# Splitting product 5 of a fast matrix product once more in the eight convolution groups

## The chip, the cores and the metric

The kernel runs on one core of a Trainium2 chip. The metric is the device time of one execution in microseconds. A profile of one execution gives the start and length of each instruction on each engine: PE (TensorE, the matmuls), DVE (VectorE), ACT (ScalarE), POOL (GpSimd) and SP (SyncE, which issues most of the DMAs). DMAs that add into their destination are issued by POOL.

## The reference, cut to what matters

```python
h = rmsnorm(x, norm_g)                       # x: 1024 tokens x 1024
proj = h @ w_in                              # 1024 x 12288
b_a, c_a, x_a, z_a, q, k, v, z_b, g_a, g_b = split(proj)
u = conv3(c_a * x_a) + conv_b                # causal, depthwise, three taps
y_a = (b_a * u * silu(z_a)) @ w_a_out
y_b = retention(q, k, v, z_b) @ w_b_out
out = rmsnorm(x + (sigmoid(g_a) * y_a + sigmoid(g_b) * y_b) @ w_o, final_g)
```

All in float32. The change concerns `h @ w_in` for the channels of the convolution branch.

## The kernel before, in words

**The product.** Each float32 operand is held as two parts, a high one rounded to the matmul's format and a low one, what is left. A product is three matmuls: high by high, high by low, low by high. `h @ w_in` is made in 2 value groups and then 20 channel groups `g` of 512 channels each: two gate groups (0, 1), eight conv groups (`CONVS`, 2 to 9), eight turn groups (`QZS`, 10 to 17: queries, keys and their gates) and two gate groups (18, 19). A channel group multiplies by a scheme with seven products of half-size matrices in place of eight (Winograd's form of Strassen's), in the order `ORDER = (1, 6, 2, 5, 7, 3, 4)`. The sums of x that it needs are made once and kept in `hc`, high and low; the sums of the weights are made for each group. A full product is 24 matmuls of 512 columns (`unit`). Products 4 (in groups 1 to 18) and 3 (in conv groups, `THIRDS`) are themselves made by the same scheme with seven quarter products: 42 matmuls of 256 columns, as `first_half` (three quarter products, 18 matmuls) and `second_half` (four, 24 matmuls). Below, 3a and 3b are the halves of product 3, 4a and 4b those of product 4. In a conv group PE does 1, 6, 2, 5, 7, 3a, 4a, 4b, 3b.

**The parts of x for a halved product.** `second_part` gives the four sums T1, T2, T3, T4. For product 4 three of them lie in `hx`, for product 3 in `third_parts`; T3 takes the place of a quarter in `hc`, and the quarter is brought back from HBM when the halved groups are over.

**Weights.** The four blocks of a group's weights (512 KB each) come into five buffers `work`, with the roles a to e of `ROLES`. SyncE loads a, b, c and d. POOL makes S1 = b + d in e (L934), S2 = a + S1 in a (L944), and S3 and S4 by adding DMAs from HBM (L939, L950). In a halved product `second_sums` makes four quarter sums in place on POOL: L957, L958, L960, L962. Each unit of work, a product or a half, has one of three `slots`: ACT copies the weights into it as the high part (`high(u)`, L1146), DVE subtracts for the low part (`low(u)`, L1678 or, without a sign change, L1681; called the split of the unit below), and PE waits for it (`w_ready`). `high(u)` waits until PE is through with unit u - 3. A first half has 768 columns of weights, all else 1024.

**Sums of the products.** Product 1 is copied out of PSUM by ACT; DVE subtracts each of 6, 5, 7, 3 and 4 (`add`, L1828 and L1830). Of a halved product DVE first does `second_first` (L1836, 256 columns, after the first half), then the three steps of `second_rest` (L1849: 768, 512 and 512 columns), then `add`. PE needs a product's bank back two products later: 3 waits for the sum of 5, 7 for the reader of 2.

**A conv group's tail.** When group g - 1 was a conv group, the work of its channels runs beside group g. ACT makes sigmoids and `first_tap`; POOL multiplies three gates (`conv_gate`: L980, L976, L983); DVE does `conv_product` for both halves (L1901, L1904), two `conv_tap` (L1909) and `conv_y` (L1916). DVE's `conv_early` (L1894, the gate product) multiplies a half of product 2 with its sigmoid straight out of PSUM, and PE's product 7 waits for it. ACT's copies out of product 2 wait for `conv_y` of the group before.

**The order** is written out by hand: each engine has a loop over the units u, and places each step by group and by place p of the unit in its group. Each engine works strictly in its own order. DVE in a conv group behind a conv group, before: at the start split 6, rest of 3, its `add`, L1901, split 2, L1904; then split 5; after product 6 `add`, taps, y, split 7; after 2 split 3a and the gate product; after 5 `add` and split 4a; after 7 `add` and split 4b; after 3a and 4a their `second_first`, split 3b and split 1 of the next group; after 4b its rest and `add`.

## Time and the profile before

| | us |
|---|---|
| median of 3 runs | 1365.0 (1364.61 to 1365.46) |
| the profiled execution | 1365.87 |
| its span, first to last instruction | 1364.1 |
| PE busy | 1351.8 |
| DVE, ACT, POOL busy | 1060.0, 608.3, 413.7 |

The granted TensorE clock is full nearly throughout (mean 0.998). Matmuls are pipelined, so the length shown for one (0.39 us for 512 columns) is more than the distance to the next (0.227 us). Conv groups lie between 238 and 536 us of the span.

### The profile page before, as it was taken

What the parts mean: (1) busy time and instruction counts of PE and PEld (TensorE: products, weight loads), DVE (VectorE), ACT (ScalarE), POOL (GpSimd) and SP (SyncE); (2) the same over time, 40 slices, a digit from 0 to 9 for tenths busy, and PEclk for the clock granted to TensorE, in tenths of its full rate; (3) what the DMA queues carried; (4) which work ended last, traced back from release to release, by engine and by line L of the source; (5) the groups of instructions that cost most, each with busy time, mean ns of one, the idle gap of its engine ahead of it and who ended that gap; (6) DMA issues with size and microseconds to landing.
All of it is one profiled execution on the core that took longest, in us unless ns stands there. A gap on an engine that the chain in (4) does not pass through costs nothing.

```text
span 1364.1 us, 17294 instructions
## 1 busy us (share of the span) xinstructions
PE 1351.8 (99%) x6642; PEld 1142.7 (84%) x6642; DVE 1060.0 (78%) x1097; ACT 608.3 (45%) x821; POOL 413.7 (30%) x381
## 2 busy tenths in 40 slices
PE   9999999999999999999999999999999999999997
PEld 7788888888888888888888888888888888888886
DVE  6898465677878777678888778748776998788887
ACT  6843233433333333333333433438778433433445
POOL 0100112344444554444443444315444001100002
PEclk9999999999999999999999999999999999999999
DMA  9646445344433433476666666757768699945443
GB/s 333 216 132 214 141 110 166 95 108 109 109 101 86 108 93 99 136 183 172 176 162 166 147 166 179 223 201 252 267 223 267 141 332 308 235 158 201 162 85 124
DMA packets 112979, 234.81 MB, mean 172 GB/s; under 512 B 7680, under 2 KB 50816, under 8 KB 108032
## 3 DMA queue, kind: packets, MB, share of 16 engines
q1 hardware_dynamic: 104112, 194.87, 42.2%
q0 software_dynamic: 8640, 38.80, 16.0%
q8 instruction: 53, 0.87, 0.3%
q14 instruction: 30, 0.25, 0.1%
q10 hardware_dynamic: 144, 0.02, 0.0%
HBM read 169.70 MB, written 55.57 MB: 165 GB/s over the span
## 4 chain that ended last, share of the span: by engine, by line
PE 92%; ACT 2%; issue 1%; DVE 1%; DMA 1%; POOL 1%; SPq 1%; POOLq 0%; ACTq 0%; DVEq 0%
PE psum L2625 15%; PE psum L2627 15%; PE psum L2628 15%; PE psum L2768 7%; PE psum L2766 7%; PE psum L2767 7%; PE psum L2549 3%; PE psum L2551 3%; PE psum L2550 3%; PE psum L2538 3%; PE psum L2540 3%; PE psum L2541 3%; PE psum L2670 2%; PE psum L2672 2%; PE psum L2671 2%
## 5 line engine op out<-in xcount | busy, mean ns | idle before, releaser
L1146 ACT ACTIVATE slots<-work 128x1024 fp32r<-128x1024 f32 (+1 forms) x166 | 169.5, 1027 | 418.0 <-PE psum L2628 292.1
L2625 PE MATMUL psum<-hc,slots 128*128 128x512 f32 x912 | 355.0, 389 | 0.0
L2627 PE MATMUL psum<-hc,slots 128*128 128x512 f32 x912 | 354.9, 389 | 0.0
L2628 PE MATMUL psum<-hc,slots 128*128 128x512 f32 x912 | 354.8, 389 | 0.0
L2628 PEld LDWEIGHTS psum<-hc,slots 128*128 128x128 f32 x912 | 171.2, 188 | 35.8
L2625 PEld LDWEIGHTS psum<-hc,slots 128*128 128x128 f32 x912 | 171.2, 188 | 35.3 <-issue 0.4
L2627 PEld LDWEIGHTS psum<-hc,slots 128*128 128x128 f32 x912 | 171.2, 188 | 34.8
L1435 ACT ACTIVATE last_slot<-arena 128x1024 fp32r<-128x1024 f32 x112 | 118.6, 1062 | 163.0 <-PE psum L2768 157.3
L2766 PE MATMUL psum<-last_slot 128*128 128x512 f32 (+1 forms) x452 | 175.3, 388 | 0.0
L2768 PE MATMUL psum<-last_slot 128*128 128x512 f32 (+1 forms) x452 | 175.0, 387 | 0.0
L2767 PE MATMUL psum<-last_slot 128*128 128x512 f32 (+1 forms) x452 | 175.0, 387 | 0.0
L2008 DVE TENSOR_TENSOR last_slot<-arena,last_slot 128x1024 fp32r<-128x1024 f32 x112 | 135.7, 1221 | 31.1 <-ACT last_slot L1435 30.4
L1681 DVE TENSOR_TENSOR slots<-work,slots 128x1024 fp32r<-128x1024 f32 x100 | 142.9, 1429 | 12.9 <-ACT slots L1146 12.7
L2767 PEld LDWEIGHTS psum<-last_slot 128*128 128x128 f32 x452 | 84.9, 188 | 17.4
L2766 PEld LDWEIGHTS psum<-last_slot 128*128 128x128 f32 x452 | 84.9, 188 | 17.4
L2768 PEld LDWEIGHTS psum<-last_slot 128*128 128x128 f32 x452 | 84.9, 188 | 17.2
L957 POOL TENSOR_TENSOR work<-work 128x256 f32<-128x256 f32 x26 | 23.4, 898 | 244.5 <-DVE slots L1678 244.5
L1828 DVE TENSOR_TENSOR tp_v<-psum,tp_first 128x1024 f32<-128x1024 f32 x40 | 48.8, 1220 | 55.5 <-PE psum L2628 55.3
L1678 DVE SCALAR_TENSOR_TENSOR slots<-work,slots 128x1024 fp32r<-128x1024 f32 (+1 forms) x66 | 74.8, 1133 | 20.9 <-ACT slots L1146 20.9
L2538 PE MATMUL psum<-slots,hc 128*128 128x512 f32 x224 | 88.3, 394 | 1.6 <-DVE slots L1681 1.6
L2541 PE MATMUL psum<-slots,hc 128*128 128x512 f32 x224 | 87.2, 389 | 0.0
L2540 PE MATMUL psum<-slots,hc 128*128 128x512 f32 x224 | 87.1, 389 | 0.0
(228 smaller groups left out, 2496.1 us busy)
## 6 DMA issues: line engine op xcount, KB each, us to landing
work<-w_channel SPq DMA_DIRECT2D x80, 512.0 KB, 4.0
work<-w_channel POOLq DMA_DIRECT2D x40, 512.0 KB, 5.5
arena<-w_last SPq DMA_DIRECT2D x19, 1024.0 KB, 7.9
qk<-qk_scratch SPq DMA_DIRECT2D x32, 512.0 KB, 3.4
arena<-w_last POOLq DMA_DIRECT2D x9, 1024.0 KB, 10.5
v_raw<-value_scratch SPq DMA_DIRECT2D x32, 256.0 KB, 3.9
arena<-gate_scratch SPq DMA_DIRECT2D x16, 512.0 KB, 6.8
value_c<-w_value SPq DMA_DIRECT2D x10, 512.0 KB, 4.8
```

Source lines behind the costliest of these rows:

```text
L1146: nc.scalar.activation(slots[:, u % SLOTS, 0, 0:columns_of(u)], src, ACT.Copy, scale=-1.0 if negated(u) else 1.0).then_inc(w_hi, 1)
L1681: nc.vector.tensor_tensor(slot[:, 1, :], src, slot[:, 0, :].bitcast(F32), ALU.subtract).then_inc(w_ready, 1)
L2008: nc.vector.tensor_tensor(slot[:, 1, :, :], pair_at(group, product, j), slot[:, 0, :, :].bitcast(F32), ALU.subtract).then_inc(last_ready, 1)
L2538: nc.tensor.matmul(bank, x_high, w_high, start=product in starts and i == 0 and kk == 0, stop=False, skip_group_check=True)
L2540: nc.tensor.matmul(bank, x_high, w_low, start=False, stop=False, skip_group_check=True)
L2541: last = nc.tensor.matmul(bank, x_low, w_high, start=False, stop=i == 1 and kk == 1, skip_group_check=True)
L2625: nc.tensor.matmul(bank, slot[:, 0, w], x_high, start=product in STARTS and j == 0, stop=False, skip_group_check=True)
L2627: nc.tensor.matmul(bank, slot[:, 0, w], x_low, start=False, stop=False, skip_group_check=True)
L2628: last = nc.tensor.matmul(bank, slot[:, 1, w], x_high, start=False, stop=j == 3, skip_group_check=True)
L2766: nc.tensor.matmul(bank, l_high, r_high, start=start, stop=False, skip_group_check=True)
L2767: nc.tensor.matmul(bank, l_high, r_low, start=False, stop=False, skip_group_check=True)
L2768: return nc.tensor.matmul(bank, l_low, r_high, start=False, stop=stop, skip_group_check=True)
```

## The change

`FIFTHS = CONVS`: product 5 of the conv groups is halved as well, as the units 5a (place 3) and 5b (`FIFTH_HALF`), which PE does one behind the other. What goes with it:

- Weights: e is now loaded by SyncE with a block of its own, and POOL adds the other block by a DMA (`s1` in groups 1 to 19), as S3 and S4 were made already. The roles d and e stay in their buffers. A group has five plain loads and three adding ones, before four and two.
- POOL's quarter sums for product 5 stand between its second and third gate product; the third gate product comes after them.
- x: the parts of product 5 are made in group 0 (`t5_quarter`, `t_sum`, `fifth_high`, `fifth_low`), stored in HBM (`hx_d`, `kept_d`) from group 1 on, and `hx` is reloaded twice in each conv group: with the parts of product 5 behind 4b of the group before, with those of product 4 behind 5b. Each reload is one DMA of 512 KB (T4) and one of 1 MB (T1 and T2). `kept_d` and the preparation of product 4's sums in group 0 move by a few places.
- DVE in a conv group behind a conv group, after: at the start split 6, rest of 3, `add`, L1901, split 2, **split 5a**, L1904; after 6 `add`, tap 1, **split 5b**, tap 2, y; after 5a **its `second_first`**, split 7, the gate product, split 3a; after 5b **the first step of its rest**, split 4a, **the two other steps**, `add`; from the `add` of product 7 on as before.
- The four low parts of product 3's x (`third_low`, in the first conv group alone): before, three at place 3 and one at place 4; now all at place 4 (the unit of product 7), where DVE comes to them behind the `add` of product 5. PE's 3a waits for the four, as before.

```diff
 THIRDS = CONVS
+FIFTHS = CONVS
+LAST_HALF, THIRD_HALF, FIFTH_HALF = 7, 8, 9
+UNIT_TABLE = [(g, p) for g in range(GROUPS) for p in (0, 1, 2, 3, FIFTH_HALF, 4, 5, 6, LAST_HALF, THIRD_HALF)
+              if (p != THIRD_HALF or g in THIRDS) and (p != LAST_HALF or g in TWICE) and (p != FIFTH_HALF or g in FIFTHS)]
...
-    ROLES.append(dict(a=r["c"], b=r["b"], c=r["a"], d=r["e"], e=r["d"]))
+    ROLES.append(dict(a=r["c"], b=r["b"], c=r["a"], d=r["d"], e=r["e"]))
...
     # SyncE
+        def load_hx(product):
+            n = int(product == 5)
+            sp.dma_start(hx[:, 2].bitcast(F32), hx_d[n, :, 2]).then_inc(t4_in, 16)
+            sp.dma_start(hx[:, 0:2].bitcast(F32), hx_d[n, :, 0:2]).then_inc(t1_t2_in, 16)
...
+            if g == 1:
+                sp.wait_ge(h_ready, made(3) + 4)
+                for part, a in enumerate((t5_high, t5_low)):
+                    sp.dma_start(hx_d[1, :, :, part], a[:, 0:3]).then_inc(fifth_kept, 16)
+                    sp.dma_start(kept_d[3, :, part], a[:, 3]).then_inc(fifth_kept, 16)
+                sp.wait_ge(fifth_kept, 112)
+                sp.wait_ge(h_ready, made(3) + 4 + 3)
+                sp.dma_start(hx_d[0], hx[:, :].bitcast(F32)).then_inc(fifth_kept, 16)
...
+            if g in FIFTHS:
+                sp.wait_ge(unit_done, ended_at(g - 1) + 1)
+                load_hx(5)
...
-                sp.wait_ge(w_ready, unit_at(g, 5) + 1)
-                load_work(g + 1, "d", 3)
+                sp.wait_ge(w_ready, fifth_ended_at(g) + 1)
+                load_work(g + 1, "e", 3)
                 sp.wait_ge(w_ready, unit_at(g, 7) + 1)
                 load_work(g + 1, "b", 2)
                 if g in THIRDS and g > THIRDS.start:
                     stores[kind_of(g - 1)](g - 1)
+                if g in FIFTHS:
+                    sp.wait_ge(unit_done, fifth_ended_at(g) + 1)
+                    load_hx(4)
+                if g in THIRDS:
+                    sp.wait_ge(w_ready, ended_at(g) + 1)
+                    load_work(g + 1, "d", 3)
...
     # POOL
         def s1(g):
...
+            if g:
+                work_loaded(g, "e")
+                pool.dma_start(work[ROLES[g]["e"]][:, :], w_channel[g, 2], accum_op=ALU.add).then_inc(s1_in, 16)
...
-                conv_gate(g - 1, 2)
...
+            if g in FIFTHS:
+                second_sums(g, 5)
+            if conv:
+                conv_gate(g - 1, 2)
             if g in THIRDS:
                 second_sums(g, 3)
...
     # DVE
+                elif n == 3 and halved_product(g, 5):
+                    second_first(g, 5)
+                elif n == FIFTH_HALF:
+                    second_rest(g, 5, range(1))
+                    low(u + 2)
+                    second_rest(g, 5, range(1, 3))
+                    add(g, 5)
...
-                for n in range(1, CONV):
+                conv_tap(place_of(u)[0] - 1, 1)
+                if place_of(u)[0] in FIFTHS:
+                    low(u + 2)
+                for n in range(2, CONV):
                     conv_tap(place_of(u)[0] - 1, n)
                 conv_y(place_of(u)[0] - 1)
...
+            elif u >= VALUE_UNITS and place_of(u)[0] in FIFTHS and place_of(u)[1] in (0, 1, 2, 3, 4, FIFTH_HALF):
+                conv = place_of(u)[0] - 1 in CONVS
+                if place_of(u)[1] == 0 or place_of(u)[1] in (1, 2) and not conv:
+                    low(u + 2)
+                if place_of(u)[1] == 0 and conv:
+                    low(u + 3)
+                if place_of(u)[1] == FIFTH_HALF:
+                    low(u + 1)
+                    if place_of(u)[0] in CONVS:
+                        conv_early(place_of(u)[0])
+                    low(u + 2)
...
-            if g == THIRDS.start and p == 3:
-                for name in ("T2", "T4", "T3"):
+            if g == THIRDS.start and p == 4:
+                for name in ("T2", "T4", "T3", "T1"):
                     third_low(name)
-            if g == THIRDS.start and p == 4:
-                third_low("T1")
...
     # PE
             product_of_quarters(u, 1, quarter(product, 2), direct_quarter(g, product, 0))
+            if product != 3 and g in FIFTHS:
+                pe.wait_ge(t4_in, 16 + 16 * hx_loads(g, product))
             product_of_quarters(u, 2, second(product, "T4"), direct_quarter(g, product, 2)).then_inc(unit_done, 1)
...
+            if product != 3 and g in FIFTHS:
+                pe.wait_ge(t1_t2_in, 16 + 16 * hx_loads(g, product))
             product_of_quarters(u, 2, second(product, "T1"), psum[:, z + 1, 0:QUARTER], start=True)
...
                     first_half(g, product)
+                    if product == 5:
+                        second_half(g, 5)
```

## Rows read from the trace of the kernel before

**Rows 1.** The page, busy us of each engine, shares of the span and instructions.
```profile
PE 1351.8 (99%) x6642; PEld 1142.7 (84%) x6642; DVE 1060.0 (78%) x1097; ACT 608.3 (45%) x821; POOL 413.7 (30%) x381
```
**Rows 2.** Windows, one conv group: length, busy us (instructions) by engine, clock, DMA.
```profile
461.70:498.90 37.20, 37.20 (x207) 32.50 (x206) 29.04 (x29) 12.79 (x15) 17.51 (x15) 1.00 0.38 97
```
**Rows 3.** Timeline of PE (start, length), where columns change: conv groups, then a turn group.
```profile
461.68 0.40 PE L2625 MATMUL psum<-hc,slots 128*128 128x512 f32 x1
...
488.90 0.28 PE L2549 MATMUL psum<-hc,slots 128*128 128x256 f32 x1
...
498.86 0.40 PE L2625 MATMUL psum<-hc,slots 128*128 128x512 f32 x1
...
568.70 0.28 PE L2549 MATMUL psum<-hc,slots 128*128 128x256 f32 x1
...
573.63 0.39 PE L2625 MATMUL psum<-hc,slots 128*128 128x512 f32 x1
```
**Rows 4.** Timeline of DVE in the same conv group, from 2.7 us before it.
```profile
459.01 2.40 DVE L1849 TENSOR_TENSOR tp_v<-tp_v,psum 128x768 f32<-128x768 f32 x3
461.52 1.22 DVE L1830 TENSOR_TENSOR tp_v<-tp_v,psum 128x1024 f32<-128x1024 f32 x1
462.75 1.23 DVE L1681 TENSOR_TENSOR slots<-work,slots 128x1024 fp32r<-128x1024 f32 x1
...
468.25 1.22 DVE L1681 TENSOR_TENSOR slots<-work,slots 128x1024 fp32r<-128x1024 f32 x1
469.38 1.78 DVE L1904 TENSOR_TENSOR u_pad<-u_pad,tp_v 128x512 f32<-128x512 f32 x1
471.09 2.32 DVE L1681 TENSOR_TENSOR slots<-work,slots 128x1024 fp32r<-128x1024 f32 x1
...
474.46 2.59 DVE L1909 SCALAR_TENSOR_TENSOR taps<-u_pad,cols,taps 128x1024 f32<-128x1024 f32 x2
...
484.81 0.95 DVE L1678 SCALAR_TENSOR_TENSOR slots<-work,slots 128x768 fp32r<-128x768 f32 x1
...
493.39 0.42 DVE L1836 TENSOR_TENSOR tp_v<-tp_v,psum 128x256 f32<-128x256 f32 x1 [1.60 <-PE psum L2551]
```
**Rows 5.** Timeline of POOL in the same group.
```profile
459.17 2.40 POOL L944 TENSOR_TENSOR work<-work,work 128x1024 f32<-128x1024 f32 x1 [1.14 <-DVE slots L1681]
...
468.35 2.27 POOL L976 TENSOR_TENSOR gate_z<-gate_z,tp_first 128x512 f32<-128x512 f32 x1 [1.88 <-ACT gate_z L1302]
470.69 1.63 POOL L983 TENSOR_TENSOR gate_z<-gate_z,tp_v 128x512 f32<-128x512 f32 x1
...
485.83 0.74 POOL L957 TENSOR_TENSOR work<-work 128x256 f32<-128x256 f32 x1 [2.49 <-DVE slots L1678]
```
**Rows 6.** Timeline of DVE and of POOL in the first conv group (start 238.29).
```profile
256.58 1.83 DVE L1882 TENSOR_TENSOR third_T<-t_sums,third_T 128x512 fp32r<-128x512 f32 x2
...
256.76 1.10 POOL L957 TENSOR_TENSOR work<-work 128x256 f32<-128x256 f32 x1 [13.56 <-DVE slots L1678]
```
**Rows 7.** Timeline of DVE and of PE where product 7 of that group begins.
```profile
259.49 0.68 DVE L1894 TENSOR_TENSOR gate_z<-psum,gate_z 128x512 f32<-128x512 f32 x1
...
259.84 0.39 PE L2628 MATMUL psum<-hc,slots 128*128 128x512 f32 x1
260.26 0.47 PE L2625 MATMUL psum<-hc,slots 128*128 128x512 f32 x1
```
**Rows 8.** Timeline of ACT at the start of the conv group of rows 3 to 5.
```profile
461.65 1.06 ACT L1146 ACTIVATE slots<-work 128x1024 fp32r<-128x1024 f32 x1 [4.38 <-POOL work L944]
```
**Rows 9.** DMA issues of the whole run: count, KB each, median us to landing.
```profile
arena<-w_last SPq DMA_DIRECT2D x19, 1024.0 KB, 7.9
...
value_scratch<-value_v SPq DMA_DIRECT2D x4, 1024.0 KB, 4.8
```
**Rows 10.** POOL's DMAs of line L939 in the conv groups.
```profile
DMA to landing us min/median/max: 6.0/6.6/7.2
```
**Rows 11.** POOL's DMAs of line L950 in the conv groups.
```profile
DMA to landing us min/median/max: 5.3/5.4/5.6
```

More of the change, by code:

```diff
@@ L342, in build @@
     t4_sums = sb("t4_sums", CONS_AT + 8 * KB, [P, 4, 2, QUARTER])
+    t5_high, t5_low = (sb(f"t5_{n}", TP_AT[1] + m * 8 * KB, [P, 4, 2, QUARTER]) for m, n in enumerate(("high", "low")))
     t3_quarters = sb("t3_quarters", CONS_AT, [P, 4, 2, QUARTER])
@@ L460, in build @@
     kept_in, third_kept = x_in[4], x_in[7]
+    fifth_kept, t4_in, t1_t2_in = x_start, x_in[5], x_in[6]
     def g_col(k):
@@ L716, in _ @@
                 stores[kind_of(g - 1)](g - 1)
+            if g + 1 < GROUPS and g not in THIRDS:
+                sp.wait_ge(w_ready, ended_at(g) + 1)
+                load_work(g + 1, "d", 3)
             if g == QZS.start:
@@ L1217, in h_high, with fifth_high @@
             nc.scalar.activation(half_kept(name, 0, i), halved(source[name], i), ACT.Copy).then_inc(h_hi, 1)
+        def fifth_high():
+            act.wait_ge(t_made, 12 + 8)
+            for n in range(4):
+                nc.scalar.activation(t5_high[:, n].bitcast(F32R), t5_low[:, n], ACT.Copy).then_inc(h_hi, 1)
         def second_high(name):
             n = ("T1", "T2", "T4", "T3").index(name)
-            act.wait_ge(t_made, 12 + 4 + (1, 3, 4, 2)[n])
+            act.wait_ge(t_made, 20 + 4 + (1, 3, 4, 2)[n])
             if name == "T3":
@@ L1547, in _ @@
             g, p = place_of(u)
-            if g == 0 and p == 5:
+            if g == 0 and p == 2:
+                fifth_high()
+            if g == 0 and p == 6:
                 for name in ("T1", "T2", "T4"):
@@ L1836, in second_first, with second_rest @@
             nc.vector.tensor_tensor(at, at, psum[:, second_bank(g, product), 0:QUARTER], ALU.subtract).then_inc(value_sum, 1)
-        def second_rest(g, product):
-            dve.wait_ge(unit_done, (ended_at(g) if product == 4 else third_ended_at(g)) + 1)
+        def second_rest(g, product, parts=range(3)):
+            dve.wait_ge(unit_done, halved_ended_at(g, product) + 1)
             z = second_bank(g, product)
             to = flat((tp_v if product == 4 else tp_first)[g % 2][:, :, :]).rearrange("p (n c) -> p n c", n=4)
-            for n, (quarters, bank, c) in enumerate(((slice(1, 4), z, 0), (slice(1, 4, 2), z + 1, 0),
-                                                     (slice(2, 4), z + 1, QUARTER))):
+            for n in parts:
+                quarters, bank, c = ((slice(1, 4), z, 0), (slice(1, 4, 2), z + 1, 0), (slice(2, 4), z + 1, QUARTER))[n]
                 if n:
@@ L2129, in _ @@
             g, p = place_of(u)
-            if g == 0 and p in (1, 2):
-                for n in range(2):
-                    t4_quarter(2 * (p - 1) + n)
-            if g == 0 and p in (3, 4):
-                for name in (("T1", "T3"), ("T2", "T4"))[p - 3]:
-                    t_sum(name, t4_quarters, t4_sums, 12)
-            if g == 0 and p == 6:
+            if g == 0 and p == 0:
+                for n in range(4):
+                    t5_quarter(n)
+            if g == 0 and p == 1:
+                for name in ("T1", "T3", "T2", "T4"):
+                    t_sum(name, t5_high, t5_low, 12)
+            if g == 0 and p == 3:
+                fifth_low()
+            if g == 0 and p in (2, 4):
+                for n in range(2):
+                    t4_quarter(p - 2 + n)
+            if g == 0 and p == 5:
+                for name in ("T1", "T3", "T2", "T4"):
+                    t_sum(name, t4_quarters, t4_sums, 20)
+            if g == 1 and p == 0:
                 for name in ("T1", "T2", "T4"):
@@ L2172, in _ @@
             if kind_of(g) == "conv":
-                if p == 3:
+                if p == 3 and g not in FIFTHS:
                     conv_early(g)
@@ L2592, in unit @@
                 pe.wait_ge(kept_in, 80)
+            if product == 5 and g == FIFTHS.stop:
+                pe.wait_ge(fifth_kept, 192)
             if product == 3 and g == THIRDS.stop:
```

125 lines of the change are left out of this document (82 added, 43 removed).

## The prediction

> **What bounds the kernel now.** The page's busy shares come first: TensorE is at work for 1351.8 of 1364.1 us [rows 1]. The table of windows then shows one conv group: PE busy all of its 37.20 us at full clock, DVE 29.04 [rows 2]. So the time is the length of the matmul stream, and it changes only if the stream gets shorter or has to wait. The timeline of PE gives lengths [rows 3]: five full products take 488.90 - 461.68 = 27.22, 5.444 each; the two halved ones 498.86 - 488.90 = 9.96, 4.98 each; a halved one alone 573.63 - 568.70 = 4.93. The group lasts 37.18. Below, t counts from the start of product 1 of a conv group; that of [rows 3 to 5] starts at 461.68.
>
> The timelines of DVE and POOL [rows 4 to 7] show who keeps PE fed. Three rules are read there. First, on DVE an op that depends on nothing recent starts 0.08 before its predecessor ends (468.25 + 1.22 = 469.47, L1904 starts at 469.38 [rows 4]). Second, DVE ops with both inputs in SBUF wait for a running POOL op: L976 ends at 468.35 + 2.27 = 470.62, and L1904, 0.69 alone, ends at 471.16, 0.54 after it; the split at 471.09 ends 1.09 after L983 [rows 4, 5]. The additions out of PSUM (459.01, beside POOL's op at 459.17) keep their 2.40. Third, the price of a late signal to PE: at 259.84 the last matmul of product 5 starts, so product 7 was due at 260.07; DVE's gate product ended at 259.49 + 0.68 = 260.17, PE went on at 260.26, with 0.47 in place of 0.39 [rows 7]. A signal 0.10 late cost 0.28; I take the lateness plus 0.19.
>
> **The gain.** Product 5 becomes 42 matmuls of 256 columns for 24 of 512, in eight groups. Each saves 5.444 - 4.93 = 0.51, or 0.46 by the pair's pace. I take 0.51: 37.18 becomes 36.67, in all 4.1 us (0.46: 3.7). The boundaries move to: 5a at t = 16.33, 5b 18.44 (18 matmuls of 0.1174), product 7 21.26, 3a 26.71.
>
> The Trainium skill, "TensorE: Matmul & The Clock Gate", section "Back-to-back issue gap", gives N/2.4 + 2.5 ns for N columns, 216 and 109 ns, by which a product would save 24 x 0.2158 - 42 x 0.1092 = 0.59 and the eight 4.7 us; the rows have 0.2268 and 0.1174, and the measurement decides.
>
> **DVE's bill.** Per group it adds 0.42, 0.95 and two of 0.69 of additions and a split of three quarters (0.95): 3.5 us, so 32.5 of 36.7. It still fits in sum; order decides. POOL gives one 2.40 sum per group to a DMA and gets four quarter sums of about 0.74 [rows 5]; DMA gets 3 MB of hx and two more blocks of 0.5 MB.
>
> **When DVE reaches product 5's first sum (call it D).** Up to the split at 468.25 (t = 6.57) nothing changes. Next comes 5a's split, at 7.71, under L976 (to 8.94): it ends at 8.94 + 0.80 = 9.74. L1904 ends at 10.28. POOL's quarter sums start only then (they wait for 5a's split, and now sit ahead of L983): 10.89, 11.6, 12.3, and the fourth at 13.1, or at 14.1 if tap 1 (ready at 12.23, after product 6's sum at 10.89 + 0.2) takes its turn first. ScalarE's copy costs 1.06 [rows 8]: 14.2 or 15.25. The split of 5b meets L983 and ends at 16.5 or 16.75. Tap 2 and y, 1.28 and 1.22, end at 18.95 or 19.2. 5a ends at 18.44, and DVE would go on at 18.64 (4a ended at 488.90 + 4.27 = 493.17, L1836 started at 493.39 [rows 3, 4]). So D is 18.85 to 19.1 where PE's own limit is 18.64. Bounds: 18.64 without any collision, 19.5 if each costs a full 1.63.
>
> **Who waits on it.** Behind D stand product 7's split (1.14), the gate product, 3a's split (0.87), first addition (0.87), 4a's split (0.87), two additions and the sum. The gate product used to be far ahead of product 7. It now ends at D + 2.16 = 21.0 to 21.3, and product 7 needs its bank at 21.26: with the 0.19, a stall of 0 to 0.2. The last three take 2.74 (461.52 + 1.22 - 460.00, where the second of the additions at 459.01 starts [rows 4]), so the sum of product 5, for which 3a waits, is done at D + 7.43: 26.3 to 26.5, against 26.71. But 3a's split releases POOL's sums for product 3 at D + 3.1, and 4a's split falls due at D + 3.82, when the second of these (D + 3.81) is just beginning. In [rows 6] DVE and POOL take turns: DVE's second op, due at 257.19, ended at 258.41, 0.55 after POOL's. If POOL is first, 4a's split ends 0.57 late, and the sum is done at 26.9 to 27.1: a stall of 0.35 to 0.6. If DVE is first, 0 to 0.2.
>
> The Trainium skill, "SBUF — State Buffer", section "Who interferes with whom", says that a DVE instruction with two SBUF inputs and a GpSimd one that reads SBUF block each other for a whole instruction, and that issue order decides. By that rule POOL, 0.01 ahead, would win and the stall would be 0.35 to 0.6; this case's trace agrees that whole instructions block ([rows 6]), but no row has a tie so close.
>
> I take 0.4 per group, between the two, in the seven conv groups behind a conv group: 2.8 us.
>
> **The first conv group** has no gates, taps or y to do, so D is 18.64, and the 0.28 stall of [rows 7] goes, as the gate product is done by 20.8. But the four low parts for product 3 are moved behind product 5's sum, and 3a waits for all. That sum ends at 26.1 to 26.7. The four parts cost 0.61 each freely and 1.15 each in turns with POOL's sums for product 4 ([rows 6]: 0.54 + 0.61), which run until about 28. Done at 28.7 to 30: a stall of 2.2 to 3.3, and I take 2.8.
>
> **Costed at nothing.** Group 0's preparation of product 5's parts (some 12 DVE ops of 0.7, four on ScalarE): products of 5.44 have one split and one sum each there, about 2.3, and splits run a product ahead. Were that cover gone, every microsecond late at a split would be one for PE. The stores of these parts make SyncE's queue wait in group 1, with weight loads behind; those are due a group later. The hx reload for product 4 (0.5 + 1 MB) is issued when 5b ends, t = 21.4, behind a weight block and y's store; the three parts after T4 are due at 3a + 4.2 = 31. 1 MB lands in 4.8 alone and 7.9 under load [rows 9]; with 2.5 MB queued, 28.5 to 31. The second product's sum S1 by DMA is treated as a rival. The turn groups keep their matmuls and lose a POOL sum each; nothing. Loads that are merely renamed (d for e) or reordered are due a group later; nothing.
>
> **The sum.** Eight conv groups now: 7 x 37.18 + 37.46 = 297.7. After: 8 x 36.67 + 2.8 + 2.8 = 299.0. That is +1.2 on the profiled execution (span 1364.1, time 1365.87, so 1.8 lie around the span); the median of the runs is 1365.0, so 1366.2 us. About 0.2%, 2.7 us, is what a measurement of this kernel can tell from no change.
>
> **Rivals.**
> *S1 late (slower).* S1 was a POOL sum with nothing to fetch; S2 ran 459.17 to 461.57, ScalarE took it at 461.65, and DVE split it at 462.75, exactly when it came free [rows 4, 5, 8]. Now S1 is a DMA issued when POOL has done product 4's quarter sums, D + 9.6. The next group starts at D + 8.0 + 0.19 + 9.96 = D + 18.2 when the chain through 3a binds, and S2 must start 2.5 ahead, so the DMA has about 6.0 us. POOL's DMAs landed in 5.3 to 5.6 [rows 11] or 6.0 to 7.2 [rows 10]. From 6.0 on each microsecond delays the whole DVE chain, and thus PE, by one per group: at 6.6, 0.6 x 7 = 4.2 more, 1370.4. For it: S3's DMA and weight loads are in flight too. Against: S1 is the first in its queue. Chance 0.2.
> *hx late (slower).* If the 1 MB takes 7.9 from the landing of its 0.5 MB (about 24), product 4's second half, due at 31, waits 1 us in eight groups: 1374; 0.4 us are enough to decide (3.2 more). For it the 3 MB per group, against it the 97 GB/s of now [rows 2]. Chance 0.08. Longer turns on POOL, D at 19.5 and POOL first: a stall of 0.98, 1370: 0.1.
> *The chain holds (faster).* DVE is first at 4a's split and D is 18.85: no stall, and 2.2 in the first group: 2.2 us faster, 1362.8, still no measurable change. Only if the first group's parts too are hidden does the whole gain of 4.4 come out, 1360.6. For it: DVE's load leaves 4 us idle per group. Against: the order of ops. 0.12 for beyond 0.2%.
> *No measurable change* by the mechanisms above: 0.50. So faster 0.12, same 0.50, slower 0.38.
>
> The likeliest case's own range is 1362.8 to 1367.7. The range takes in S1 late by 0.6 and the better case: 1362.0 to 1371.5.
>
> **What would show it.** Right: the conv groups last 37.0 to 37.3; product 5 runs at 0.117 per matmul; PE waits before 3a (released by DVE's L1830 of product 5) and a little before 7; one wait of 2 to 3 us before 3a in the first conv group, released by L1882; 5a's split stretched to 2. Wrong: groups of 36.7, with no wait; or waits at product 6 (S2) or inside product 4 (DMA of hx), above 37.6. The forecast fails if POOL's ops are much shorter beside DVE, or if DMA is late where no row shows it.

## The result, and the profile after

The changed kernel takes 1368.62 us, the median of 8 runs (1367.7 to 1370.51); the kernel before, beside it, 1364.92 (8 runs, 1364.1 to 1365.46). The ratio is 1.0029, with a 95% interval of 1.0018 to 1.004: slower by 0.29%, 3.7 us. The forecast was 1366.2 in a range of 1362.0 to 1371.5. The profiled execution took 1369.39 with a span of 1367.6, against the 1364.1 of before.

The page after, busy us of each engine, the row that answers to [rows 1]:
```profile
PE 1352.3 (99%) x6786; PEld 1148.5 (84%) x6786; DVE 1090.5 (80%) x1149; ACT 616.7 (45%) x833; POOL 414.4 (30%) x413
```
PE has 144 matmuls more, eight groups of 42 - 24, and is no less busy than before: the page alone does not say that product 5 became shorter. The windows do. They are cut where PE's first product begins: the first conv group, the seven conv groups behind it, and the nine stretches from there to the last group (before, the same three: 37.48, 260.26 and 338.30):
```profile
237.97:280.70 42.73, 39.30 (x225) 35.21 (x224) 28.30 (x33) 14.88 (x19) 15.72 (x17) 0.92 0.78 233
280.70:539.20 258.50, 258.50 (x1557) 230.99 (x1556) 218.39 (x232) 94.50 (x106) 144.31 (x133) 1.00 0.69 210
539.20:877.89 338.69, 338.69 (x1677) 287.50 (x1675) 276.73 (x287) 128.47 (x158) 130.95 (x107) 1.00 0.73 193
```
Those rows place the whole difference. The first conv group is 42.73 - 37.48 = 5.25 longer, the seven others together are 1.76 shorter (36.93 each against 37.18), the turn groups 0.39 longer; the region starts 0.32 sooner and the rest is 0.06 shorter, which gives +3.5. So the change pays 1.8 us in seven groups and loses three times that in one place. The column before the last two is the granted clock: 0.92 in the first group.

**The first conv group.** The timeline of PE, of DVE and of POOL where product 3's first half begins:
```profile
264.46 0.39 PE L2763 MATMUL psum<-hc,slots 128*128 128x512 f32 x1
268.29 0.55 PE L2676 MATMUL psum<-hc,slots 128*128 128x256 f32 x1 [3.43 <-DVE third_T L1982]
```
```profile
262.82 1.23 DVE L1914 TENSOR_TENSOR tp_v<-psum,tp_first 128x1024 f32<-128x1024 f32 x1
263.96 1.92 DVE L1982 TENSOR_TENSOR third_T<-t_sums,third_T 128x512 fp32r<-128x512 f32 x2
265.81 1.21 DVE L1982 TENSOR_TENSOR hc<-t_sums,hc 128x512 fp32r<-128x512 f32 x1
266.94 1.21 DVE L1982 TENSOR_TENSOR third_T<-t_sums,third_T 128x512 fp32r<-128x512 f32 x1
```
```profile
264.16 1.17 POOL L1030 TENSOR_TENSOR work<-work 128x256 f32<-128x256 f32 x1
...
266.54 1.05 POOL L1034 TENSOR_TENSOR work<-work 128x256 f32<-128x256 f32 x1
```
The sum of product 5 ends at 264.05. The four low parts follow and alternate with POOL's quarter sums until 268.15: the first part takes 0.79, each of the three others 1.21 where 0.69 is its time alone, and POOL's ops take 1.05 to 1.17 for 0.74. 3a was due at 264.69 and starts at 268.29: 3.60 lost. A second loss comes behind it. The windows over the wait and after it:
```profile
264.60:268.20 3.60, 0.25 (x2) 0.00 (x0) 3.60 (x5) 1.15 (x2) 3.52 (x5) 0.82 0.35 146
268.20:270.90 2.70, 2.61 (x12) 2.64 (x13) 2.21 (x2) 0.54 (x1) 1.11 (x2) 0.50 0.72 94
270.90:273.60 2.70, 2.70 (x15) 2.70 (x14) 0.42 (x1) 1.06 (x1) 0.00 (x0) 0.50 1.01 190
273.60:278.00 4.40, 4.40 (x39) 4.40 (x39) 2.69 (x3) 1.06 (x1) 0.00 (x0) 0.99 0.83 196
```
From 268.2 to 273.6 the granted clock is 0.50, that is 1.2 GHz, and 2.70 us hold 15 matmuls of 256 columns where full clock would hold 23. PE counts as busy throughout. Products 3 and 4 together take 280.70 - 268.29 = 12.41 here and 9.95 at full clock in the groups of the kernel before (9.96 in [rows 3]): 2.46 us more. The group thus pays 3.60 + 2.46 = 6.06 for one late operand.

**A conv group behind another.** The timeline of PE in the group that starts at 465.30, at the start of product 4's second half, 4b:
```profile
496.21 0.28 PE L2678 MATMUL psum<-hx,slots 128*128 128x256 f32 x1
496.45 0.39 PE L2676 MATMUL psum<-hx,slots 128*128 128x256 f32 x1
```
The starts lie 0.24 apart where 0.12 is the pace, and the next pair (496.45 to 496.67) loses as much again: products 3 and 4 take 10.19 for 9.95. So 0.24 is lost, and this is the only wait of the group; before 3a there is none. DVE and POOL around it, rows that answer to [rows 4, 5]:
```profile
484.20 0.41 DVE L1922 TENSOR_TENSOR tp_first<-tp_first,psum 128x256 f32<-128x256 f32 x1
...
488.00 0.95 DVE L1764 SCALAR_TENSOR_TENSOR slots<-work,slots 128x768 fp32r<-128x768 f32 x1
...
490.38 1.23 DVE L1914 TENSOR_TENSOR tp_v<-psum,tp_first 128x1024 f32<-128x1024 f32 x1
...
495.17 1.22 DVE L1764 SCALAR_TENSOR_TENSOR slots<-work,slots 128x1024 fp32r<-128x1024 f32 x1 [1.71 <-ACT slots L1223]
```
```profile
487.30 0.74 POOL L1029 TENSOR_TENSOR work<-work 128x256 f32<-128x256 f32 x1 [6.63 <-DVE slots L1764]
488.00 1.55 POOL L1030 TENSOR_TENSOR work<-work 128x256 f32<-128x256 f32 x1
...
493.25 0.74 POOL L1034 TENSOR_TENSOR work<-work 128x256 f32<-128x256 f32 x1
...
499.82 2.40 POOL L1016 TENSOR_TENSOR work<-work,work 128x1024 f32<-128x1024 f32 x1 [4.10 <-DMA work<-w_channel]
```
D is 484.20, t = 18.90. The tie that the prediction turned on is the pair at 488.00: 4a's split took 0.95, the POOL op beside it 1.55. DVE went first, and product 5's sum ends at 491.61 (t = 26.31), before 3a is due. The same pair two groups earlier, which starts at 391.46:
```profile
414.15 1.56 POOL L1030 TENSOR_TENSOR work<-work 128x256 f32<-128x256 f32 x1
...
414.16 0.95 DVE L1764 SCALAR_TENSOR_TENSOR slots<-work,slots 128x768 fp32r<-128x768 f32 x1
```
Here POOL's op starts 0.01 ahead, as the prediction had it, and DVE's goes free all the same. So it is in all seven groups: the two starts are at the same hundredth or POOL's one ahead, DVE's op takes 0.95 and POOL's 1.55 to 1.56.

The wait at 4b follows from POOL: 3a's split releases product 3's quarter sums at t = 22.0, product 4's end at 493.99 (28.69), ScalarE copies, and the split of 4b ends at 496.39 where PE wanted it at 496.33. POOL's row at 499.82 shows the other thing that was new: S2 waits for S1's DMA.

### The profile page after: what moved, and what is told of

It reads as the page before. It is cut to its first block, busy times and chain, and to the rows that moved or that the text cites. A ratio compares the mean times of both kernels' runs of the same rounds, so it can differ in the third digit from the quotient of the medians.

```text
span 1367.6 us, 17788 instructions
## 1 busy us (share of the span) xinstructions
PE 1352.3 (99%) x6786; PEld 1148.5 (84%) x6786; DVE 1090.5 (80%) x1149; ACT 616.7 (45%) x833; POOL 414.4 (30%) x413
## 4 chain that ended last, share of the span: by engine, by line
PE 90%; DVE 3%; ACT 2%; issue 2%; DMA 1%; POOL 1%; SPq 1%; POOLq 0%; ACTq 0%; DVEq 0%
PE psum L2760 14%; PE psum L2762 14%; PE psum L2763 14%; PE psum L2903 7%; PE psum L2904 7%; PE psum L2905 7%; PE psum L2676 4%; PE psum L2678 4%; PE psum L2677 4%; PE psum L2665 3%; PE psum L2668 3%; PE psum L2667 3%; PE psum L2805 2%; PE psum L2807 2%; PE psum L2806 2%
## 5 line engine op out<-in xcount | busy, mean ns | idle before, releaser
L1223 ACT ACTIVATE slots<-work 128x1024 fp32r<-128x1024 f32 (+1 forms) x174 | 175.2, 1017 | 387.9 <-PE psum L2763 180.1
L2760 PE MATMUL psum<-hc,slots 128*128 128x512 f32 x848 | 330.2, 389 | 0.0
L2762 PE MATMUL psum<-hc,slots 128*128 128x512 f32 x848 | 330.1, 389 | 0.0
L2763 PE MATMUL psum<-hc,slots 128*128 128x512 f32 x848 | 330.0, 389 | 0.0
L2763 PEld LDWEIGHTS psum<-hc,slots 128*128 128x128 f32 x848 | 159.2, 188 | 33.2
L2760 PEld LDWEIGHTS psum<-hc,slots 128*128 128x128 f32 x848 | 159.2, 188 | 32.8 <-DVE slots L1767 0.4
L2762 PEld LDWEIGHTS psum<-hc,slots 128*128 128x128 f32 x848 | 159.2, 188 | 32.0
L1767 DVE TENSOR_TENSOR slots<-work,slots 128x1024 fp32r<-128x1024 f32 x108 | 148.3, 1379 | 30.1 <-ACT slots L1223 29.9
L1029 POOL TENSOR_TENSOR work<-work 128x256 f32<-128x256 f32 x34 | 31.2, 918 | 223.8 <-DVE slots L1764 214.7
L2676 PE MATMUL psum<-hc,slots 128*128 128x256 f32 x272 | 77.6, 285 | 3.4 <-DVE third_T L1982 3.4
## 6 DMA issues: line engine op xcount, KB each, us to landing
arena<-w_last POOLq DMA_DIRECT2D x9, 1024.0 KB, 10.6
```

The costliest lines, as they stand in the source:

```text
L1223: nc.scalar.activation(slots[:, u % SLOTS, 0, 0:columns_of(u)], src, ACT.Copy, scale=-1.0 if negated(u) else 1.0).then_inc(w_hi, 1)
L1767: nc.vector.tensor_tensor(slot[:, 1, :], src, slot[:, 0, :].bitcast(F32), ALU.subtract).then_inc(w_ready, 1)
L2676: nc.tensor.matmul(to, slot[:, 0, w], high, start=start and j == 0, stop=False, skip_group_check=True)
L2760: nc.tensor.matmul(bank, slot[:, 0, w], x_high, start=product in STARTS and j == 0, stop=False, skip_group_check=True)
L2762: nc.tensor.matmul(bank, slot[:, 0, w], x_low, start=False, stop=False, skip_group_check=True)
L2763: last = nc.tensor.matmul(bank, slot[:, 1, w], x_high, start=False, stop=j == 3, skip_group_check=True)
```

## The experiments

Eleven kernels were run. Times are medians with their range where there are several runs, else that of a single run; "conv region" is from the first conv group to the first turn group (before 297.74), "turn region" from there to the last group (before 338.30), both read from PE's timeline.

### Three of the four low parts early
On the changed kernel, three of the four low parts go back to where the kernel before has them:
```diff
-            if g == THIRDS.start and p == 4:
-                for name in ("T2", "T4", "T3", "T1"):
+            if g == THIRDS.start and p in (3, 4):
+                for name in (("T2", "T4", "T3",), ("T1",))[p - 3]:
                     third_low(name)
```


> The changed kernel with the low parts of product 3's x back where they were (T2, T4, T3 at place 3, T1 at place 4). Theory A, the first conv group pays: the wait before 3a there (3.6 us) shrinks to 0.2 to 0.6, because one part is left behind product 5's sum, and the 2.4 us of half clock behind it go too; 5.6 us less than the changed kernel, about 1363.0, 0.1 to 0.2% faster than before. Theory B, the clock is lost for another reason (the load of the changed schedule): only the wait goes, 3.2 less, about 1365.4, and a stretch of half clock stays. Theory C, the cost is spread over all groups (DMA, POOL): hardly anything changes, 1368.

Measured: 1364.89 us (11 runs, 1363.8 to 1366.24), before beside it 1364.99; ratio 1.0 (0.9991 to 1.0009). The span fell from 1367.6 to 1363.0. The windows from the same place, over the former wait and to the end of the group:
```profile
264.60:268.20 3.60, 3.55 (x29) 3.23 (x28) 1.53 (x3) 1.14 (x2) 3.52 (x5) 1.00 0.27 112
264.60:275.23 10.63, 10.58 (x86) 10.16 (x85) 8.12 (x11) 3.07 (x3) 6.20 (x6) 1.00 0.75 170
```
The wait shrank to 0.21 and the clock stayed at 1.00. This one edit takes back 3.7 us, all that the change had lost. The first group came down by 5.57 (42.73 to 37.16), which is what theory A had; the span fell by 1.0 less than that, as the turn groups are 0.5 longer than in the changed kernel and two conv groups last 37.20 and 37.02. The medians lie 3.7 apart and not 4.6 because the profiled execution of the changed kernel was 0.8 above its median. What is left is a conv region of 296.05, 1.7 better than before, and a turn region of 339.18, 0.9 worse.

### The same four parts late in the kernel before, and how the loss grows
The kernel before with all four parts behind product 5's sum; the changed kernel with two, and with three of them late:
```diff
-            if g == THIRDS.start and p == 3:
-                for name in ("T2", "T4", "T3"):
-                    third_low(name)
             if g == THIRDS.start and p == 4:
-                third_low("T1")
+                for name in ("T2", "T4", "T3", "T1"):
+                    third_low(name)
```


> The kernel before with one thing changed: all four low parts of product 3's x at place 4, behind product 5's sum and 4a's split. There product 5 is whole, its sum ends at t = 23.1 and 4a's split at 24.0 of the first conv group, and 3a is due at 27.5. Theory A: the four parts take turns with POOL's sums for product 4 at 1.15 each, are done at 28.6 to 29, and PE waits 1.0 to 1.6 before 3a; the 0.28 before product 7 goes, as the gate product is no longer behind three parts. Without a fall of the clock +0.9 us (1365.9), with one +3 (1368). Theory C: no difference from before.

> The changed kernel with two of the four parts (T3, T1) behind product 5's sum. Theory A: the wait before 3a is about 1.5 us. Whether the clock falls after 1.5 us of waiting is what this run is to show: if the fall needs a longer wait, the halves behind it run at 0.1185 per matmul and the group costs 1.5 more than in e1 at most; if any wait will do, 2.4 come on top. Theory B: half clock as in the changed kernel.

> The changed kernel with three of the four parts (T4, T3, T1) behind product 5's sum. Theory A: the wait before 3a is 2.3 to 2.8 us, 0.8 to 1.2 less than in the changed kernel. With a clock that falls only behind a long wait, this run lies near the point: either full clock (wait alone) or 2.4 us of half clock on top.

Measured, in this order: 1366.0 (10 runs; ratio 1.0008, 0.9998 to 1.0017), and in one run each 1366.47 and 1368.68. PE's first matmul of 3a in the three:
```profile
266.20 0.36 PE L2547 MATMUL psum<-hc,slots 128*128 128x256 f32 x1 [0.87 <-DVE third_T L1882]
```
```profile
265.37 0.36 PE L2676 MATMUL psum<-hc,slots 128*128 128x256 f32 x1 [1.18 <-DVE third_T L1982]
```
```profile
266.85 0.35 PE L2676 MATMUL psum<-hc,slots 128*128 128x256 f32 x1 [2.31 <-DVE third_T L1982]
```
Against the pace the three waits cost 1.03, 1.33 and 2.46, the first and the last in the ranges that were expected, the second a little under the 1.5. After the first two the clock stays full and the pair of products takes 10.02 and 10.03. After the third the windows show it low:
```profile
266.70:268.70 2.00, 1.85 (x10) 1.88 (x11) 1.36 (x3) 1.06 (x1) 2.00 (x3) 0.64 0.00 0
268.70:272.00 3.30, 3.30 (x22) 3.30 (x21) 1.43 (x2) 1.06 (x1) 0.32 (x1) 0.70 0.99 160
```
and the pair takes 11.52, 1.57 more. So the loss at 3a is the wait; a wait of 1.33 us brought nothing on top of it here, one of 2.46 us a second loss. Moving the four parts alone, in the kernel before, costs only 1.0: there they begin at 261.94, t = 23.99, where the changed kernel begins them at 25.99, and 3a is due half a microsecond later in the group (t = 27.2 for 26.7).

The trace of the kernel with two parts late shows something else as well. In the conv group that starts at 460.16, S2 and the row before product 7:
```profile
459.12 2.40 POOL L1016 TENSOR_TENSOR work<-work,work 128x1024 f32<-128x1024 f32 x1 [5.51 <-DMA work<-w_channel]
```
```profile
482.70 0.47 PE L2760 MATMUL psum<-hc,slots 128*128 128x512 f32 x1 [0.81 <-DVE gate_z L1994]
```
S1's transfer was some 1.4 us later than in the other groups (4.10 in the changed kernel's row), S2 with it, and PE lost 1.3 in that group. That is the rival "S1 late", in one group of eight.

### Is it hx? No reload, and S1 earlier
Two kernels on top of the one with three parts early. In one hx is not reloaded; it leaves out the parts of x for product 5, which is then computed from product 4's:
```diff
-            if g in FIFTHS:
-                sp.wait_ge(unit_done, ended_at(g - 1) + 1)
-                load_hx(5)
...
-                if g in FIFTHS:
-                    sp.wait_ge(unit_done, fifth_ended_at(g) + 1)
-                    load_hx(4)
```


> On top of the kernel with three low parts early: hx is not loaded again in the conv groups for product 5 and for product 4, so 24 MB of transfers less; product 5's halves read product 4's hx, so that part of the computation is changed. Theory (4b waits for its split on DVE): the 0.24 us wait at the start of 4b stays, released by DVE; span within 1 us of that kernel's 1363.0. Rival (the reload, 7.9 us long, holds 4b, or its traffic makes S1 and the quarter sums late): the wait at 4b goes, the turn groups' waits too, and the span falls by 2 to 3 us.

In the other S1 goes ahead of the quarter sums, not in the conv groups alone, as the expectation says, but in all groups of `TWICE`, 1 to 18:
```diff
+            if g + 1 < GROUPS and g in TWICE:
+                s1(g + 1)
             if g in THIRDS:
                 second_sums(g, 3)
...
             if g + 1 < GROUPS:
-                s1(g + 1)
+                if g not in TWICE:
+                    s1(g + 1)
```


> On top of the kernel with three low parts early: in the conv groups POOL issues the next group's S1 ahead of both rows of quarter sums, about 6 us sooner; the sums keep their order. Theory: the 0.24 us wait at the start of 4b stays in each conv group (its split's quarter sums have not moved), S2's wait for its DMA (23.8 us in all in the changed kernel) goes, and so do the waits at product 6 in the turn groups (0.2 to 0.5 each): about 0.9 us under the kernel that it is built on, 1364.0 us. Rival (S1 late costs nothing anywhere): the same time as that kernel, 1364.9. Rival (S1's DMA in time with the quarter sums slows them or the hx reload): slower than 1365.5.

Measured: without the reload 1364.7 (one run), span 1362.9, conv region 296.04: the same as with it. The wait at 4b is still there, 0.22, without any transfer of hx:
```profile
490.81 0.28 PE L2672 MATMUL psum<-hx,slots 128*128 128x256 f32 x1
491.05 0.39 PE L2670 MATMUL psum<-hx,slots 128*128 128x256 f32 x1
```
With S1 early, 1376.65 (4 runs, 1374.92 to 1378.25; ratio 1.0085, 1.0071 to 1.0099). The turn region is at 338.29, so the waits at product 6 there are gone, as the theory had it; its time and that of the first rival fell. The second rival, a collision with the reload, stands, and cost far more than expected. PE at 4b in the group that starts at 350.90:
```profile
382.99 0.28 PE L2681 MATMUL psum<-hx,slots 128*128 128x256 f32 x1
385.81 0.36 PE L2679 MATMUL psum<-hx,slots 128*128 128x256 f32 x1 [2.54 <-DMA hx<-hx_scratch]
```
and POOL's issue of S1, with the landing of hx's 1 MB, issued at 372.7:
```profile
371.41 0.89 POOL L996 DMA_DIRECT2D work<-w_channel  x1 [5.13 <-DMA work<-w_channel]
```
```profile
DMA to landing us min/median/max: 12.9/12.9/12.9
```
S1, waiting for its first load, went out one microsecond ahead of hx's reload and ran beside it. The reload landed after 12.9 us, and after 10.3 to 11.0 in the six other groups that waited; in the changed kernel the same reload, that for product 4, takes 7.7 to 8.0 in all eight groups. Product 4 waits for it in seven of the eight groups, 1.1 to 2.7 us at a time (in one the profile names a split on DVE instead, but that had ended 1.9 us before, and hx landed 11.0 us after its issue), and two of these groups ran on at half clock. The prediction's rival "hx late" is thus real, but only beside another transfer; the order in the change, with S1 issued 6.8 us behind the reload (493.93 and 487.14), keeps clear of it. A third kernel has both edits:

> S1 early in the conv groups, as in the kernel that was 11.7 us slower, but without the reloads of hx; product 5's halves read product 4's hx, so that part of the computation is changed. Theory (there hx's 1 MB landed in up to 12.9 us because S1's transfer ran beside it, and 4b's second operand was late): all the waits of 1.1 to 2.7 us inside product 4 go, 4b's wait falls back to 0.24 by its split, and the span is at 1362 to 1363.5. Rival (S1's place in GpSimd's queue, where it holds up the quarter sums while it waits for its own load, is what cost the time): the waits stay, released by DVE, and the span stays above 1370.

Measured: 1362.73 (one run), span 1360.9, conv region 295.64, turn region 338.29. All the long waits are gone, 4b keeps its 0.24. So they came from the two transfers together, and not from S1's place in GpSimd's queue. Like the kernel without reloads, this one computes product 5 from the wrong parts of x: it shows a cause and is no version to use.

### What holds 4b
Product 4's quarter sums ahead of product 3's, with S1 between them:
```diff
-            if g in THIRDS:
-                second_sums(g, 3)
+            if g + 1 < GROUPS and g in TWICE and g not in THIRDS:
+                s1(g + 1)
             if g in TWICE:
                 second_sums(g, 4)
+            if g + 1 < GROUPS and g in THIRDS:
+                s1(g + 1)
+            if g in THIRDS:
+                second_sums(g, 3)
...
```


> On top of the kernel with three low parts early: POOL sums product 4's quarters before product 3's, and in the conv groups issues the next group's S1 between the two (ahead of product 4's where there is no product 3). Theory (4b's split is late because its quarter sums come behind product 3's): 4b's split is done at about t = 29.3 instead of 31.1, the 0.24 us wait at the start of 4b goes in all conv groups, they last 36.67 to 36.7 instead of 36.9, S2 waits for no DMA, and the small waits at product 6 in the turn groups go: 8 x 0.24 + 0.9 = about 2.8 us under the kernel that it is built on, so 1362 us, 0.2% faster than before. Rival (hx reload is what holds 4b): the wait stays at 0.24 and the time is 1364 to 1365.

Measured: 1366.55 (11 runs, 1365.73 to 1367.18; ratio 1.0011, 1.0002 to 1.002). The turn region is back at 338.29 and the wait at 4b is gone, as expected; yet six groups last 37.5. PE and DVE's gate product before product 7, then DVE and POOL ahead of the next group, which starts at 498.80:
```profile
482.49 0.28 PE L2683 MATMUL psum<-hx,slots 128*128 128x256 f32 x1
483.16 0.47 PE L2765 MATMUL psum<-hc,slots 128*128 128x512 f32 x1 [0.40 <-issue]
```
```profile
482.38 0.68 DVE L1999 TENSOR_TENSOR gate_z<-psum,gate_z 128x512 f32<-128x512 f32 x1
...
494.54 1.23 DVE L1769 SCALAR_TENSOR_TENSOR slots<-work,slots 128x1024 fp32r<-128x1024 f32 x1 [0.90 <-ACT slots L1228]
495.68 1.22 DVE L1772 TENSOR_TENSOR slots<-work,slots 128x1024 fp32r<-128x1024 f32 x1
```
```profile
497.05 2.41 POOL L1016 TENSOR_TENSOR work<-work,work 128x1024 f32<-128x1024 f32 x1 [2.85 <-DVE slots L1772]
```
Product 4's sums can't start before 4a's split, 2 us behind 3a's, so GpSimd starts them at t = 24.4 where it started product 3's at 22.0, and product 3's sums end 6 us later than they did. The split of 3b ends at 495.77, the next split behind it at 496.90, and S2 starts 1.75 us ahead of the group instead of 2.41. DVE's chain is late by that, the gate product ends at 483.06, and product 7 starts at 483.16 where it was due at 482.61: with the slow start behind it 0.67 per group. Another 0.14 goes at the start of 3b. Taking 0.24 away at one split put more than that at two others.

### S1 later, and S1 on GpSimd
S1 behind S3 in the queue, nothing else:
```diff
             if g + 1 < GROUPS:
-                s1(g + 1)
                 s3(g + 1)
+                s1(g + 1)
```


> On top of the kernel with three low parts early: S1 is issued behind S3 in POOL's queue instead of ahead of it, nothing else. S3's transfers landed 3.5 us later than S1's, so S1 would land at least 3 us later. Theory (S1 is just in time: S2 waits for it already and the split of product 6 is due at once): S2 comes 3 to 4 us later, split 6 and DVE's chain behind it with it, and PE waits at product 6 or 7 in every group: 2 to 4 us per conv group, 1 to 3 in a turn group, in all 20 to 60 us more than that kernel's 1365. Rival (S1's transfer is hidden with room to spare): under 3 us more.

Measured: 1425.55 (one run), 60.7 more, half of it in the conv region (326.48 for 296.05). POOL and PE in one group:
```profile
308.15 1.20 POOL L996 DMA_DIRECT2D work<-w_channel  x1
318.47 2.38 POOL L1016 TENSOR_TENSOR work<-work,work 128x1024 f32<-128x1024 f32 x1 [9.12 <-DMA work<-w_channel]
```
```profile
321.12 0.39 PE L2763 MATMUL psum<-hc,slots 128*128 128x512 f32 x1
324.23 0.47 PE L2760 MATMUL psum<-hc,slots 128*128 128x512 f32 x1 [2.71 <-DVE slots L1767]
```
In second place the transfer landed after 8.9 to 10.6 us (S1 in first place, in the changed kernel: 5.3 to 5.8), S2 came some 4 us late (4.9 in this group), and 15 of the 17 groups 2 to 18 paid 1.5 to 3.6 at product 6. The room that S1 has in the conv groups is small: the prediction's decision point, 6.0 us, was right. The kernels with S1 first in the queue behind the quarter sums bear it out. In their conv groups S1 is issued 8.3 us ahead of the next group. Where it landed after 5.9 or less, PE lost nothing before product 7; six landings of 6.05, 6.07, 6.16, 6.99, 7.03 and 7.21 cost 0.13, 0.15, 0.24, 1.07, 1.09 and 1.26, each time the landing less 5.9.

S1 summed by GpSimd again, in every group or in the turn groups only (with `g > CONVS.stop` for `g`):
```diff
             if g:
+                a, b, c, d, e = buffers(g)
                 work_loaded(g, "e")
-                pool.dma_start(work[ROLES[g]["e"]][:, :], w_channel[g, 2], accum_op=ALU.add).then_inc(s1_in, 16)
+                work_loaded(g, "b")
+                nc.gpsimd.tensor_tensor(e, b, e, ALU.add).then_inc(s1_in, 16)
```


> On top of the kernel with three low parts early: S1 is summed by GpSimd in place in every group behind group 0, so that the conv groups give GpSimd 2.4 us back. Theory (GpSimd's place ahead of 4b's and 3b's splits is taken: its quarter sums end at t = 28.7, S1 would run from there to 31.2 and block the split of 4b on DVE): 4b waits 1.3 to 1.6 us more in each conv group, 10 to 13 us in all, 1375 to 1378. Rival (GpSimd has room, S1 needed no DMA): the time stays within 1 us of 1364.9. [...]

> On top of the kernel with three low parts early: for the groups 11 and on, S1 is summed by GpSimd in place (e plus b) as it was in the kernel before, not added by a DMA; the conv groups keep the DMA. Theory (the turn groups lost their 0.2 to 0.9 us because S2 waited for S1's DMA): S2 waits for no DMA there, the waits at product 6 in the turn groups go and the turn region takes its 338.3 us again instead of 339.2: about 0.5 us under the kernel that it is built on in the median, 1364.4. Rival (it is the traffic of the transfers, or DVE, that makes them late): the turn region stays at 338.7 or more and the time at 1364.9.

Measured: in every group 1371.25 (one run), 6.4 more. PE at 4b, and DVE and POOL:
```profile
459.68 0.38 PE L2683 MATMUL psum<-hx,slots 128*128 128x256 f32 x1 [0.99 <-DVE slots L1771]
```
```profile
457.37 2.26 DVE L1771 SCALAR_TENSOR_TENSOR slots<-work,slots 128x1024 fp32r<-128x1024 f32 x1 [1.70 <-ACT slots L1230]
```
```profile
456.14 2.41 POOL L998 TENSOR_TENSOR work<-work,work 128x1024 f32<-128x1024 f32 x1
```
GpSimd's 2.41 block the split of 4b, 1.22 alone, to 2.26; 4b waits 1.1 to 1.2 in all eight groups, 1.0 more than with the DMA, where 1.3 to 1.6 more was expected. So in the conv groups the DMA for S1 is worth 1.0 us each, and in the turn groups the sum on GpSimd is the better choice: with it there alone 1363.46 (11 runs, 1362.53 to 1364.71), before beside it 1364.84, ratio 0.9991 (0.9982 to 1.0). The turn region is back to the hundredth:
```profile
534.67:872.97 338.30, 338.30 (x1677) 287.72 (x1675) 272.49 (x287) 128.06 (x158) 156.80 (x107) 1.00 0.68 181
```
This is the best version found, 1.4 us under the kernel before, which is less than the 0.2% that a measurement of this kernel can tell from no change. Its profiled execution still has one conv group in which S1's transfer was late: S2 waited 5.30 for it there and 3.9 to 4.4 in the others, and PE lost 1.07.

## Why the prediction was right or wrong

**The gain: right.** Product 5 runs at 0.1174 per matmul and takes 4.93, 5.45 - 4.93 = 0.52 less than a full one; the 0.59 that the formula quoted in the prediction would give did not come. A group without waits would last 36.67.

**DVE's chain to D: right.** D is 18.90 for 18.85 to 19.1. GpSimd's quarter sums came after 5a's split, tap 1 took its turn before the fourth, and no wait of note stands before product 7. 5b's split ended at 16.53 for 16.5 or 16.75. DVE's bill was set too high: it is busy for 218.39 / 7 = 31.2 us of a group, not 32.5, among other things because the second half of `conv_product` no longer meets a POOL op (0.68 for the 1.78 of L1904 in [rows 4]).

**0.4 before 3a in seven groups, 2.8 us: wrong, it was nothing.** The step that failed is the tie at 4a's split. Its two sides were worked out, 0 to 0.2 if DVE is first, and DVE was first in all seven. The Trainium skill, "SBUF — State Buffer", section "Who interferes with whom", has issue order decide who blocks; this trace agrees that one of the two blocks for a whole instruction (POOL's 0.74 became 1.55), but if the order is read from the starts, it does not bear out the rest: POOL's op was 0.01 ahead at 414.15 and at the same hundredth at 488.00, and DVE's went first each time. What decides a tie this close is not shown.

**4b: a term that was missing.** The prediction followed DVE's signals up to the sum of product 5 and hx's transfer to t = 31, but not GpSimd's sums on to 4b's split. Product 4's sums began at t = 24.15 [rows 5]; now they begin at 25.7, behind product 3's, and PE reaches 4b 0.5 sooner. The price is 0.24 in each group. That it is this split and not hx is shown: the wait stays when the reloads are gone, and goes when the sums of product 4 are made first.

**The first conv group: the place right, the size wrong, one mechanism missing.** The stall by L1882's successor before 3a was forecast at 2.2 to 3.3 and measured at 3.60. The term that was too small is the end of the four parts, given as 28.7 to 30 and measured at t = 30.18: they began at t = 26.0 and three of them took 1.21, a start every 1.13, in turns with POOL's sums, which ran until t = 29.6 and not until 28. 3a starts 0.14 behind the last of them. The 2.46 us of half clock behind the wait had no term at all. Together the group came to 42.73 where the prediction has 36.67 + 2.8 = 39.47.

**The sum.** The first group 3.3 too low, the seven others 0.14 each too high (37.07 for 36.93), the turn groups 0.39 and the start -0.32: +1.2 became +3.5. The forecast of "no measurable change" missed by the half clock; taken off the medians' difference, 3.7 - 2.46, it leaves +1.2, inside 0.2%. That this is the number that was forecast is luck: the first wait was 0.8 longer than the term for it, 4b cost 1.7 in seven groups and the turn groups 0.39, and against these stood 2.8 us before 3a that never came. It is partly luck too that 1368.6 lies in the range: the range was widened for S1 late, and what used the room was the half clock.

**Costed at nothing.** Group 0's preparation and the renamed loads: nothing, right (the conv region starts 0.32 sooner). The hx reload: nothing as it stands, shown by taking it out. The turn groups: wrong by a little. "Lose a POOL sum each; nothing" overlooked that what replaces the sum is a transfer in front of S2. It lands after 6.9 to 7.7 us there (5.3 to 5.8 in the conv groups; why it takes longer is open), S2 waits 5.2 to 6.0 for it in seven turn groups, and product 6's split is at times late: 0.39 in the profile after, 0.88 in that of the kernel with three parts early, nothing when the sum is back on GpSimd, and nothing when the transfer is issued ahead of the quarter sums (338.29 in all three kernels that do so).

**The rivals.** "S1 late" was described rightly and is on the edge: it does not decide in most groups, appears in single ones (six groups of five kernels, 0.13 to 1.26 us a time, none in the changed kernel's own trace), and decides everything once the transfer is second in its queue. "hx late" did not occur, and does as soon as another transfer runs beside it. "The chain holds" was half right: it held in seven groups.

Left open: in which share of executions a conv group is hit by a late S1. The runs of the kernel with three parts early spread over 2.4 us (1363.8 to 1366.24), which such groups would explain, but only profiled executions show them.

## What to carry to other kernels

A late operand has two prices, the wait and, if the wait is long enough, slower matmuls behind it; when a stall is forecast for a busy TensorE that is as long as those after which the clock fell here (1.93 us and more), add a term for the second or break the stall up. When work is moved, follow every engine that it pushes until its last consumer: here GpSimd's sums mattered at 4b, one split beyond where the prediction stopped, and swapping two of its jobs only moved the lateness to 3b and product 7. A sum given to a DMA frees an engine but puts a transfer in front of the next step, which is worth it only in the groups where the engine is short, and only away from other transfers that have a due time.

## What the runs showed of the hardware

**The clock behind a wait.** All waits of 1.0 to 1.75 us in the conv and turn groups, 19 of them over these runs, were followed by full clock (one had a second wait of 2.70 right behind it, and the clock fell after that). Of the longer ones some were followed by half clock (1.2 GHz) for 2.8 to 5.4 us, costing 1.1 to 2.5: 1.93, 2.46, 2.70, 2.88, 2.99, 3.23, 3.60 and 3.63. Others were not, in the kernel with S1 behind S3: 1.91, 2.30, 2.65 and five of 3.22 to 3.55. The windows behind a wait of 2.88, one of 2.65 and one of 3.55, all in that kernel:
```profile
325.60:328.20 2.60, 2.60 (x8) 2.00 (x7) 2.49 (x3) 1.27 (x3) 0.72 (x2) 0.51 0.98 181
408.00:410.70 2.70, 2.70 (x12) 2.23 (x13) 2.53 (x4) 0.01 (x1) 1.53 (x2) 1.00 0.64 97
732.70:735.30 2.60, 2.57 (x11) 2.15 (x12) 2.60 (x2) 2.06 (x4) 2.22 (x2) 1.00 0.30 33
```
So the length of the wait alone does not tell whether the clock falls: 1.93 and 1.91, 3.23 and 3.22 went different ways. What else decides is not shown.

**Two DMAs behind each other on GpSimd's queue.** Both of 512 KB and issued 0.6 us apart. In the conv groups the first landed in 5.2 to 5.8 us and the second in 8.9 to 10.3, whichever of S1 and S3 it was (the changed kernel with S1 first, the other order with S3 first). In most turn groups of the same two kernels the first took 6.8 to 8.0 and the second 10.1 to 10.6. Issued 0.4 to 1.1 us ahead of the reload of hx, in the kernel with S1 early, S1 took 8.1 to 11.1.
